# Two weight slabs in buffers of their own behind h3 and h4, w_out summed in one PSUM bank pair, half tiles turned a slab sooner, and x2 normalised ahead of a slab

## What is computed

```python
h = x                                                     # x = first_block(...): ends in an rmsnorm
f = swiglu(rms_norm(h, ffn1_pre_g), ffn1_w_gu, ffn1_w_down)        # "f2i", "f2o"
h = h + 0.5 * rms_norm(f, ffn1_post_g)                             # "h3"
z = rms_norm(h, mix_pre_g) @ w_in                                  # "in2"
...                                                       # o_na: 8 neighbourhood heads, o_mla: 8 latent heads
mixed = jnp.concatenate([rms_norm(o_na, na_out_norm_g),
                         rms_norm(o_mla, mla_out_norm_g)], axis=-1) @ w_out   # "out2"
h = h + rms_norm(mixed, mix_post_g)                                # "h4"
f = swiglu(rms_norm(h, ffn2_pre_g), ffn2_w_gu, ffn2_w_down)        # "f3i", "f3o"
h = h + 0.5 * rms_norm(f, ffn2_post_g)
```

## Time and profile before

| what | us |
|---|---|
| median of 3 runs | 973.73 (972.49 to 975.08) |
| the profiled execution | 973.97 |
| its span, first to last instruction | 972.1 |
| PE busy in the span | 948.7 |
| mean granted TensorE clock | 0.998 of full |

### The profile page before, as it was taken

One profiled execution on the slowest core, in us unless ns is written; L12 is line 12 of the kernel. 1 busy time (PEld: TensorE's weight loads), 2 busy tenths in 40 slices (PEclk: granted clock), 3 DMA queues, 4 the chain that ended last, 5 costly groups with the idle time before them and its releaser, 6 DMA issues.

```text
span 972.1 us, 14450 instructions
## 1 busy us (share of the span) xinstructions
PE 948.7 (98%) x4870; PEld 803.2 (83%) x4870; DVE 512.9 (53%) x851; ACT 490.1 (50%) x771; POOL 293.7 (30%) x152
## 2 busy tenths in 40 slices
PE   8999999999999999999999999989999989999997
PEld 7999988888888888888788888878888768888886
DVE  5858955556754434423844443357477863344332
ACT  6577455644464444444645444446346554544442
POOL 1000000000043443444434434634312034434442
PEclk9999999999999999999999999999999999999999
DMA  7755565345556666886566655645502446556662
GB/s 238 242 176 173 168 194 175 127 147 176 175 173 183 187 192 197 259 235 180 172 204 186 191 174 193 193 138 176 181 2 87 128 137 206 178 175 195 186 189 78
DMA packets 132770, 169.32 MB, mean 174 GB/s; under 512 B 16707, under 2 KB 88430, under 8 KB 132598
## 3 DMA queue, kind: packets, MB, share of 16 engines
q1 hardware_dynamic: 132566, 168.67, 56.4%
q10 hardware_dynamic: 160, 0.07, 0.0%
HBM read 167.61 MB, written 1.10 MB: 174 GB/s over the span
## 4 chain that ended last, share of the span: by engine, by line
PE 89%; DVE 6%; ACT 2%; issue 2%; POOL 0%; DVEq 0%; POOLq 0%; ACTq 0%
PE acc L802 24%; PE acc L804 24%; PE acc L803 24%; PE tp L875 4%; PE acc L857 3%; PE acc L859 3%; PE acc L861 3%; DVE w_lo L1208 2%; PE sc L951 1%; PE acc L1143 1%; ACT junk L475 1%; ACT w_hi L469 1%; DVE xt_lo L1615 1%; PE tp L971 0%; DVE pt L1744 0%
## 5 line engine op out<-in xcount | busy, mean ns | idle before, releaser
L469 ACT ACTIVATE w_hi<-w_raw 128x1024 fp32r<-128x1024 f32 x305 | 322.0, 1059 | 361.0 <-PE acc L804 320.4
L1208 DVE TENSOR_TENSOR w_lo<-w_raw,w_hi 128x1024 fp32r<-128x1024 f32 x199 | 255.6, 1291 | 298.1 <-ACT w_hi L469 296.8
L1829 POOL TENSOR_TENSOR w_lo<-w_raw,w_hi 128x1024 fp32r<-128x1024 f32 x106 | 258.0, 2434 | 400.2 <-ACT w_hi L469 400.2
L802 PE MATMUL acc<-w_hi,xt_hi 128*128 128x512 f32 (+1 forms) x752 | 299.0, 398 | 5.9 <-DVE w_lo L1208 2.8
L804 PE MATMUL acc<-w_lo,xt_hi 128*128 128x512 f32 (+1 forms) x752 | 293.4, 390 | 0.0
L803 PE MATMUL acc<-w_hi,xt_lo 128*128 128x512 f32 (+1 forms) x752 | 292.8, 389 | 0.0
L802 PEld LDWEIGHTS acc<-w_hi,xt_hi 128*128 128x128 f32 x752 | 141.4, 188 | 36.0 <-DVE w_lo L1208 3.6
L804 PEld LDWEIGHTS acc<-w_lo,xt_hi 128*128 128x128 f32 x752 | 141.4, 188 | 29.6
L803 PEld LDWEIGHTS acc<-w_hi,xt_lo 128*128 128x128 f32 x752 | 141.6, 188 | 27.4
L802 PE MATMUL acc<-w_hi,hid_hi 128*128 128x512 f32 x264 | 103.2, 391 | 0.0
L804 PE MATMUL acc<-w_lo,hid_hi 128*128 128x512 f32 x264 | 102.8, 389 | 0.0
(11 more groups left out here) (210 smaller groups left out, 887.4 us busy)
## 6 DMA issues: line engine op xcount, KB each, us to landing
w_raw<-in_ffn_w_gu SPq DMA_DIRECT2D x176, 256.0 KB
w_raw<-in_w_in SPq DMA_DIRECT2D x68, 512.0 KB
w_raw<-in_w_ffn_in SPq DMA_DIRECT2D x88, 256.0 KB
w_raw<-in_ffn_w_down SPq DMA_DIRECT2D x44, 512.0 KB
w_raw<-in_w_ffn_out SPq DMA_DIRECT2D x22, 512.0 KB
w_raw<-in_w_rnn_out SPq DMA_DIRECT2D x8, 512.0 KB
w_raw<-in_w_attn_out SPq DMA_DIRECT2D x8, 512.0 KB
w_raw<-in_w_o SPq DMA_DIRECT2D x8, 512.0 KB
```

What stands on the lines that cost most here:

```text
L469: act.activation(w_hi[:, b, :], w_raw[:, b, :], ACT.Copy).then_inc(hi_done[b], 1)
L802: pe.matmul(o, hi[:, k, rows], wh, start=first and n == 0, stop=False)
L1208: dve.tensor_tensor(w_lo[:, b, :], w_raw[:, b, :], w_hi[:, b, :].bitcast(F32), ALU.subtract).then_inc(lo_done[b], 1)
L1829: pool.tensor_tensor(w_lo[:, b, :], w_raw[:, b, :], w_hi[:, b, :].bitcast(F32), ALU.subtract).then_inc(lo_done[b], 1)
```

## The change

It has five parts.

1. **Own buffers.** `AUX = 2` slabs, the first two of in2's first group and the first two of f3i's, leave the ring. They have `aux_raw`, `aux_lo` and `aux_hi` over the memory of `mqT` and `mkT`, whose heads are not in use then, and their own semaphores. The first pair is loaded behind slab 10 of f2o and copied and subtracted behind slab 17 (`feed_aux(0, 832)`); the second pair is loaded when the last scores are done, and fed after slab 7 of w_out.
2. **Feeds moved.** On ACT and DVE one ring slab instead of two is fed ahead of each row tile's split, and on DVE it stands behind `add_normed`, in the new `finish`.
3. **Half tiles.** The first row tile of h3 and of h4 is turned by halves, each half one slab sooner or at the same slab as before.
4. **w_out in one bank pair.** o_na and o_mla are multiplied by their roots (`scale_values`, L1818 of the changed kernel) before they are turned, at heads 13 and 14 for o_na. Both halves of w_out then add up in the same banks, and `gained` reads them once.
5. **f2i.** `normed_x2` comes ahead of slab 5 on DVE, the squares of x2 ahead of slab 6 on ACT, and slabs 5 and 7 are subtracted by DVE instead of POOL. The first hidden tile comes ahead of slab 7 in all FFNs.

```diff
+AUX = 2
...
-            ("in2", 4), ("uq", 2), ("ukv", 2), ("na", 1), ("mla", 1), ("top", 2), ("bot", 2), ("f3i", FG), ("f3o", 2)])
-MQK_AT, ONA_AT = 4, 10
+            ("in2", 4), ("uq", 2), ("ukv", 2), ("na", 1), ("mla", 1), ("out2", 2), ("f3i", FG), ("f3o", 2)])
+MQK_AT, ONA_AT = 4, 13
...
-        return q % 2 == 0 or q < S["f1i"] or S["in2"] <= q < S["in2"] + 4 or S["out2"] + 4 <= q < S["f3i"] + 4
+        return q % 2 == 0 or q < S["f1i"] or q in (S["f2i"] + 5, S["f2i"] + 7) or S["in2"] + AUX <= q < S["in2"] + 4 or S["out2"] + 4 <= q < S["f3i"] + 4
...
+            def load_aux_f3i():
+                sp.wait_ge(scores2, 16)
...
+            ffn_out(a["ffn1_w_down_2"][0], S["f2o"], after={10: load_aux_in2})
...
+            def feed_aux(turn, width):
+                for q in range(AUX):
+                    act.wait_ge(aux_landed[q], (16, 48)[turn])
+                    act.activation(aux_hi[:, q, 0:width], aux_raw[:, q, 0:width], ACT.Copy).then_inc(aux_hi_done, 1)
...
-                feed(s_in + 6, 1)
                 after_first()
-                feed(s_in + 7, 1)
+                feed(s_in + 6, 2)
...
-                {(1, 9): lambda: new_tile(X["h3"], 0, 0)}, by_tile=4)
+                {(1, 8): lambda: turn_new_h(X["h3"], 0, 0, 0), (1, 9): lambda: turn_new_h(X["h3"], 0, 1, 0)}, by_tile=4)
...
-                    wait_both_drained(pe, G["na"])
+                    pe.wait_ge(na_scaled, MT)
                     turn_tiles(X[f"ona{k}"], o2[:, 0], (2 * k, 2 * k + 1))
...
-                        if (m, c, q) == (1, 1, 0):
-                            new_tile(X["h4"], 4, 0)
+                        out2_products(1, c, q, (m,))
+                        if (m, c, q) in ((1, 0, 1), (1, 1, 0)):
+                            turn_new_h(X["h4"], 0, c, 4)
...
+            def finish(name, m, g, row, last_slabs, done):
+                mean_square(name, m)
+                gained(name, g + 1, 1, row, last_slabs[1], (m,))
+                for c in range(2):
+                    wait_drained(dve, g + c, m)
+                add_normed(name, m, done, lambda m, c: f[:, m, c * W:(c + 1) * W])
...
+            def scale_values(name, which, done):
+                dve.wait_ge(rs_done, NTH[name])
+                for m in range(MT):
+                    dve.tensor_scalar(o2[:, which, m, :], o2[:, which, m, :], rs[:, ST[name], m:m + 1], None,
+                                      ALU.mult).then_inc(done, 1)
...
-            feed(S["out2"], 4)
+            feed(S["out2"], 2)
             rstd("na")
-            feed(S["out2"] + 4, 2)
+            feed(S["out2"] + 2, 2)
             rstd("mla")
```

## The result

| | before | after |
|---|---|---|
| median of 4 runs each on the same chip, us | 974.4 (972.49 to 975.18) | 963.0 (962.58 to 963.55) |
| ratio to before, with its 95% interval | | 0.9888 (0.9874 to 0.9901) |
| the profiled execution, us | 973.97 | 962.92 |
| its span | 972.1 | 961.1 |
| PE busy in the span | 948.7 | 945.8 |

The change makes the kernel 11.4 us faster by the medians, 11.05 by the two profiled executions. The forecast was 964.0, with a range of 961.2 to 968.5. First the page of the changed kernel: the engines' busy time, as in the earlier trace rows, and the chain that ended last.

What follows compares the result with a forecast made beforehand. PE was taken as the bound, busy 948.7 of 972.1 us, so only its holes could be won. Gains of 11.7 us less 1.9 lost made 9.8 off 973.97: 964.2, or 963.9 by the median, stated as 964.0; range 961.2 to 968.5.

Steps and rivals of the forecast that it cites:

- f2i: Second FFN, first hidden tile: a tiny DVE coefficient stalled under POOL's subtraction; PE's hole closes, -1.7 us (-1.2 to -1.8).
- h3: Down product into in2: h comes ahead of DVE's slabs, half turns and own slabs ready; -3.9 us (-2.5 to -4.5).
- Heads: Neighbourhood heads to w_out's start: scaling o before its turn and a POOL subtraction over nm of head 14 cost +1.9 us.
- the hole ahead of ona0: In the heads: PE stands from 743.35 until the scales of o end at 745.6, nm being held until 744.1.
- h4: From w_out's first matmul to row tile 1 of f3i: 36.8 us becomes 31.1, -5.7 us (-4 to -6.1).
- clock term: Behind the 2.36 us hole around h4: 1.4 us of that gain, from a granted clock of 0.57 over 780 to 784.
- Behind it: Group 1 of f3i: the 2.3 us coefficient may stay but ends 3 us before PE wants hid; -0.4 us.
- No collision in the heads: Rival, 18%: POOL's subtraction misses nm in the heads, 1.8 of the 1.9 us go; 962.2 us.
- The heads' holes slow the clock: Rival, 17%: PE's idle 2.2 and 1.1 us before w_out lower the clock, costing 1.4 or 2.8 us; 965.5 to 967.
- The row chains are longer: Rival, 13%: half turns and the slabs behind h each 0.5 us late; 967 us, or 968 with late own-slab loads.
- it doesn't do what it says: Rival, 4%: normalisation alone, not slabs before it, holds h3 and h4, so little is won; about 972 us.
- Slower: Rival, 2%: the clock falls in the heads and stays down through w_out, eating the gain; up to 986 us.

Runs made afterwards that it cites:

- f2i_pool: Changed kernel with slabs 5 and 7 of the second FFN's first group subtracted by POOL again, new order kept; 962.84 us.
- look_a: The kernel before, unchanged, profiled a second time in one execution; 972.28 us.
- pool_late: Changed kernel with one more wait: POOL subtracts w_out's slab 2 only when DVE has done all sixteen nm; 961.31 us.
- look_b: The kernel before, unchanged, profiled a third time in one execution; 973.6 us.
- h_first: Kernel before with one edit: DVE's two ring slabs of in2 put behind the adding to h3 instead of ahead; 972.46 us.
- no_own: Changed kernel without own buffers (AUX = 0): first two slabs of in2 and f3i in the ring again, fed on DVE behind h; 967.89 us.
- aux_ahead: Changed kernel with DVE's subtractions of the two own slabs of in2 put just ahead of adding to h; 965.38 us.

## Why the prediction was right

**f2i, -1.7 forecast, -1.69 measured.** The times of the steps came within 0.1 us (coefficients done at 474.2 forecast, 474.05 measured; hid at 477.2 and 477.27). The stall was read rightly. What cures it was read only in part: the step "The change gives slabs 5 and 7 of this group to DVE, so no POOL subtraction runs here" names what happens and not what is needed, and "Moving the squares past a slab on ACT alone brings nothing" looks at the second square only and misses that the move holds back slab 7's copy and with it POOL. f2i_pool, in which nothing else differs in this stretch, closes the hole.

**h3, -3.9 forecast, -4.03 measured** (184.53 to 180.50). h came at 644.55, which is 646.15 less the 1.6 won before; the half turn at 645.36 was due at 645.3. The timelines of DVE in the changed kernel, for the earlier trace rows:

```profile
644.55 1.41 DVE L1671 SCALAR_TENSOR_TENSOR h<-f,rs,h 128x512 f32<-128x512 f32 x2
645.89 1.22 DVE L1261 TENSOR_TENSOR w_lo<-w_raw,w_hi 128x1024 fp32r<-128x1024 f32 x1
```

The holes that stay are 0.29 and 0.27 where I had 0.45 and 0.3. The loads of the own slabs were hidden: nowhere around slab 11 of f2o does ACT wait for a DMA in the trace.

**Heads, +1.9 forecast, +0.8 measured.** The mechanism was right and one term was mis-sized: the hole ahead of ona0. The forecast counts in times of the kernel before, and the changed kernel had won 5.65 us by here (in2's first group ends at 659.94 instead of 665.59). With these added, head 11's turn starts at 736.87 (736.9 forecast), PE is ready for ona0 at 743.54 (743.35), but the turn of ona0 starts at 744.48 and not at 745.6. From there to w_out it is 5.74 us (744.57 - 738.83), forecast 5.75. So all of the 1.1 us lie ahead of ona0.

The hole was to be 2.25 us (745.6 - 743.35) and is 0.94, for two reasons: the scales took 0.87 us and not 1.5, and PE was ready 2.3 us after POOL's start (737.89 against 735.62) and not 1.65. These make it 1.3 us smaller; 0.2 of them went because PE came to it 0.2 later than forecast. The hole ahead of ona1 was to be 1.1 and is 0.82, though the stretch around it is no shorter.

In holes the +0.8 looks like this. Three go, which PE's timeline of the kernel before shows:

```profile
737.22 0.63 PE L875 MATMUL tp<-ident,sb 128*128 128x128 f32 x4 [0.63 <-DVE pt L1744]
...
740.24 0.63 PE L875 MATMUL tp<-ident,o 128*128 128x128 f32 x4 [0.69 <-DVE xt_lo L1221]
...
743.54 0.63 PE L875 MATMUL tp<-ident,sb 128*128 128x128 f32 x4 [0.54 <-DVE xt_lo L1221]
```

They are 1.86 us together; after the change there are 0.70 at 731.22, 0.94 and 0.82, 2.46 together. That is 0.6 more, and 0.2 lies between the holes. The forecast names neither the three that go nor the one at 731.22, yet its times hold both: 749.43 was read with the three in it, and head 11's turn was put at 736.9, where the slot of 2.15 us alone gives 733.83 + 2.15 = 735.98. The prediction does not say where these 0.9 us come from, and the number was right.

The Trainium skill ("VectorE: DVE Perf Modes", Mode 2×_2P — use both read ports for one tensor) states that an fp32 tensor_scalar within SBUF gives two results a cycle, and the prediction's estimate from it was some 0.4 us for such a scale. The trace agrees better with it than with the 0.75 taken from PSUM: 0.473 to 0.487. The 963.2 us that went with the estimate stand beside 963.0, which is in part luck, since the scales are only one of the two reasons above.

**h4, -5.7 forecast, -5.74 measured,** from 36.79 to 31.05. Half 0 of h was turned 20.18 us after w_out's first matmul (764.75 - 744.57), forecast 20.1. But 1.1 us of this is a clock that falls in some executions of the kernel before and not in others; I had called it 1.4 and certain. Without the fall the same piece gains 4.56, where the forecast without its clock term is 4.3. So the 5.7 was met because the profile it was read from, and is compared with here, is one with the fall; that part is luck.

**Behind it, -0.4 forecast, -0.47 measured.** The coefficient is as long as forecast, under POOL, and harmless. DVE's timeline of the changed kernel:

```profile
781.34 2.36 DVE L1616 SCALAR_TENSOR_TENSOR coef<-rs 128x2 f32<-128x2 f32 x1
...
784.41 0.87 DVE L1589 SCALAR_TENSOR_TENSOR hid<-u,coef,acc 128x256 f32<-128x256 f32 x2
```

hid ends 1.4 us ahead of the turn at 786.69.

**The sum.** 9.8 forecast, 11.1 in the two profiled executions; nearly all of the difference is the heads' term. Against a profile of the kernel before without the fall (look_a) the gain is 9.9, with a heads' term 1.1 too dear and a clock term of 1.4 that is not there. Two side remarks of the prediction do not fit its rows, without touching the sum: DVE has instructions under 0.17 us (the first coefficient, 128x2, took 0.16 at 475.77 in the kernel before), and by the pitches of 0.42 and 0.23 in the earlier trace rows a microsecond of full-rate matmuls costs some 0.8 more at the low clock, not one more.

**The rivals.** *No collision in the heads* did not happen, and pool_late shows what it is worth: 1.4 us, not 1.8. *The heads' holes slow the clock* did not happen in the profile: the view by stretches of the changed kernel shows 1.00 where PE was busy 2.32 of 4 us, and 1.00 after h4, for the earlier trace rows.

```profile
738.00:742.00 4.00, 2.32 (x18) 2.00 (x19) 3.61 (x8) 2.77 (x10) 0.00 (x0) 1.00 0.60 220
...
776.00:780.00 4.00, 4.00 (x19) 3.25 (x18) 2.21 (x6) 2.66 (x5) 2.73 (x2) 1.00 0.30 103
```

After look_a and look_b this is weaker evidence than it seems, since one profile shows one execution; but the four timed runs lie within 1 us. *The row chains are longer* and *it doesn't do what it says* fell by the distances. *Slower* needed the clock to stay down through w_out, of which no trace shows a sign.

## What to carry to other kernels

When a small instruction is stretched because another engine's long one covers it, find out what releases the long one: a copy or a wait that holds it back by a microsecond removes the stall as taking the work off that engine does, and nothing was seen to be lost by it here (f2i_pool, pool_late). A slab that stands ahead of a row's chain on one engine moves its wait behind the chain when it is moved; what pays is a buffer that lets the slab be done long before (h_first against no_own). And before a clock fall goes into a sum, profile the unchanged kernel more than once, and compare by distances between rows of one stretch rather than by whole times.

## What the runs showed of the hardware that was not expected

The same hole in the same program is followed by a fallen clock in one execution and not in the next (0.57, 1.00 and 0.61 over 780 to 784 in three profiles of the kernel before). At the program's start something like it happens: in h_first, aux_ahead and pool_late the granted clock fell within the first 20 us, and the turn of h2 came at 456.44, 457.02 and 457.05 us instead of 454.7 to 455.6. The view by stretches of pool_late:

```profile
10.00:15.00 5.00, 5.00 (x33) 5.00 (x32) 1.28 (x2) 0.47 (x2) 0.00 (x0) 0.70 0.97 309
```

That execution took 963.18 us, the other three of this kernel 961.23 to 961.35. At the start, though, the holes themselves differ between executions, as PE waits there for its first inputs and slabs: behind its first matmuls the longest was 1.72 and 1.78 us in h_first and pool_late, 1.27 in aux_ahead, and at most 1.22 in the ten profiles without a fall. Much of the scatter of such a kernel may be this; only the profiled executions show it.

A scale of 128x512 (tensor_scalar, float32) on DVE took 0.48 us from SBUF to SBUF (L1818 of the changed kernel), and 0.75 from PSUM (L1777 of the kernel before).
